# Latent projections of a diffusion trunk in another order, with norm work per kind

## The reference, cut to what matters

```python
def rmsnorm(x, g):
    y = xf * lax.rsqrt(jnp.mean(xf * xf, axis=-1, keepdims=True) + EPS)
    return (y * g.astype(jnp.float32)).astype(x.dtype)

def mla_queries(p_q, q_norm_g, w_uq):
    q = (rmsnorm(p_q, q_norm_g) @ w_uq).reshape(B, L, MLA_HEADS, QK_NOPE + QK_ROPE)

def mla_keys_values(p_kv, kv_norm_g, w_ukv):
    c_kv, k_rope = p_kv[..., :KV_LORA], p_kv[..., KV_LORA:]
    kv = (rmsnorm(c_kv, kv_norm_g) @ w_ukv).reshape(B, L, MLA_HEADS, QK_NOPE + V_DIM)
```

## Time and profile before

| What | Value |
|---|---|
| Median of 3 runs | 3062.06 us (3060.01 to 3062.21) |
| The profiled execution's own time | 3062.36 us |
| Its span in the profile | 3060.6 us |
| Mean granted TensorE clock | 0.928 of full |
| TensorE busy (matrix instructions) | 2575.2 us, 84% of the span |
| VectorE, ScalarE, GpSimd busy | 847.7, 610.4, 538.4 us |
| Latent projections, layer 0 | 528.0 to 613.0 us of the span |
| Latent projections, layer 1 | 1984.8 to 2056.7 us of the span |

### The profile page before, as it was taken

One profiled execution on the slowest core, in us unless ns is written; L12 is line 12 of the kernel. 1 busy time (PEld: TensorE's weight loads), 2 busy tenths in 40 slices (PEclk: granted clock), 3 DMA queues, 4 the chain that ended last, 5 costly groups with the idle time before them and its releaser, 6 DMA issues. The chain is left out here.

```text
span 3060.6 us, 33600 instructions
## 1 busy us (share of the span) xinstructions
PE 2575.2 (84%) x12474; PEld 1499.8 (49%) x12474; DVE 847.7 (28%) x1633; ACT 610.4 (20%) x1186; POOL 538.4 (18%) x500
## 2 busy tenths in 40 slices
PE   6987977899999995988888569789999869889881
PEld 2434655545565544555554244555544445555551
DVE  3553257134100135211111142614300341111113
ACT  3332210134100011211111131004300112111111
POOL 0000011046200001222221120106500012222222
PEclk8999998999999997999989789889999979999996
DMA  9663112001013325999999422102033469999992
GB/s 332 244 251 126 69 62 65 2 12 48 21 41 104 129 89 218 388 400 396 396 385 376 176 104 75 70 10 52 7 82 96 177 268 390 395 397 400 399 359 107
DMA packets 206731, 590.78 MB, mean 193 GB/s; under 512 B 47328, under 2 KB 104715, under 8 KB 156332
## 3 DMA queue, kind: packets, MB, share of 16 engines
q1 hardware_dynamic: 183029, 557.75, 48.9%
q0 software_dynamic: 22944, 31.52, 3.2%
q10 hardware_dynamic: 663, 0.27, 0.0%
HBM read 584.07 MB, written 51.51 MB: 208 GB/s over the span
## 5 line engine op out<-in xcount | busy, mean ns | idle before, releaser
L1907 PE MATMUL ps<-wgu,moe_xt 128*64 128x256 f32 x4096 | 512.8, 407 | 122.9 <-DMA wd<-in_w_down_e 120.5
L1907 PEld LDWEIGHTS ps<-wgu,moe_xt 128*64 128x64 f32 x4096 | 336.0, 146 | 256.0 <-issue 143.6
L1486 PE MATMUL ps<-u,w_merge 128*128 128x512 f32 (+1 forms) x768 | 281.8, 525 | 4.0 <-DVEq L1503 4.0
L2000 POOL DMA_INDIRECT rows_out<-moe_rows_out,table x128 | 118.6, 927 | 788.2 <-DVE moe_rows_out L2059 768.4
L1915 PE MATMUL ps<-wd,moe_ht 128*64 128x512 f32 x1024 | 247.8, 605 | 1.5 <-DVE moe_ht L2101 1.5
L2095 DVE TENSOR_TENSOR moe_gated<-ps,moe_gated 64x256 f32<-64x256 f32 x128 | 54.5, 426 | 594.9 <-ACT moe_gated L2078 581.6
L796 PE MATMUL ps<-u,w_hy 128*128 128x512 f32 (+1 forms) x576 | 209.4, 521 | 5.6 <-PEq L127 5.6
L1486 PEld LDWEIGHTS ps<-u,w_merge 128*128 128x128 f32 x768 | 146.8, 191 | 135.1 <-issue 123.6
L1243 POOL TENSOR_SCALAR attn_p<-attn_p,attn_rs 128x768 f32<-128x768 f32 (+1 forms) x80 | 155.3, 1949 | 81.3 <-DVE attn_rs L1412 80.9
L2078 ACT ACTIVATE moe_gated<-ps 64x256 f32<-64x256 f32 x128 | 48.2, 376 | 602.5 <-PE ps L1907 578.5
L2059 DVE COPY moe_rows_out<-ps 64x512 f32<-64x512 f32 x128 | 88.7, 693 | 267.1 <-PE ps L1915 267.1
(11 more groups left out here) (313 smaller groups left out, 3028.1 us busy)
## 6 DMA issues: line engine op xcount, KB each, us to landing
wgu<-in_w_gate_e SPq DMA_DIRECT2D x128, 1024.0 KB
wgu<-in_w_up_e SPq DMA_DIRECT2D x128, 1024.0 KB
wd<-in_w_down_e SPq DMA_DIRECT2D x128, 1024.0 KB
prep_w<-in_w_ada SPq DMA_DIRECT2D x24, 2048.0 KB
w_merge<-in_w_in SPq DMA_DIRECT2D x32, 512.0 KB, 5.2
w_hy<-in_w_in SPq DMA_DIRECT2D x6, 2048.0 KB
transfer<-prep_out POOLq DMA_DIRECT2D x10, 1024.0 KB, 9.4
h<-transfer SPq DMA_DIRECT2D x4, 2048.0 KB, 11.4
```

The source lines that it names most:

```text
L1486: last = nc.tensor.matmul(m.ps[:, bank, 0:n], w[:, b, w_at + c], z[:, c, at:at + n], start=c == 0, stop=c == kn - 1)
L1907: last = nc.tensor.matmul(ps[k * SLOTS:(k + 1) * SLOTS, 0:DE], xt[:, c], wgu[:, k, c], start=c == 0, stop=c == KC - 1)
L2000: nc.gpsimd.indirect_dma_start(out=dram["y"], out_offset=bass.IndirectOffsetOnAxis(ap=m.table[0:SLOTS, j:j + 1], axis=0), in_=y[:, j % 2], ...
```

## The change

The units come in the order key-values, queries, rotary key (`order`), and banks go by the place in that order. The key-values' sums stand after the first query unit, their rows after the last query unit. The rotary key's latent half comes next, then the queries' sums, then its context half, then the queries' rows. ScalarE takes one root per kind: that of the key-values between the second and the third query unit, that of the queries last. VectorE does mean, reciprocal root and diagonals of the key-values, then their normalised product, then the rotary key's latent part, then mean, reciprocal root and diagonals of the queries, the rotary key's context copies, and the queries' normalised product. The loads on SyncE's queue and the copies on GpSimd are as before.

```diff
--- before.py
+++ after.py
@@ -1027,6 +1027,7 @@
     NU = QC + KVC + 1
     tiles_of = [sum(n for _, _, n in streams_q) // P, TT]
     turns = [(k, j) for k in (1, 0) for j in range(tiles_of[k])]
+    order = (*range(QC, QC + KVC), *range(QC))
     src = w_in[l].rearrange("(c p) n -> p c n", p=P)
     w, w_loaded = early
     wv, wv_in = values
@@ -1035,6 +1036,8 @@
                [("wkr", [P, KC, P]), ("raw", [P, QC + KVC, TOK]),
                 ("sq", [P, QC + KVC, TOK]), ("r", [P, sum(tiles_of)]), ("var", [P, sum(tiles_of)]), ("tmp", [P, sum(tiles_of)]),
                 ("diag", [P, sum(tiles_of), P]), ("t", [P, 2, SEQ]), ("g", [P, QC])]) as (block, s):
+        NQ = tiles_of[0]
+
         def streams(i):
             return streams_q if i < QC else both
 
@@ -1067,7 +1070,7 @@
             def sums(k):
 
                 first, past = ((0, QC), (QC, QC + KVC))[k]
-                pe.wait_ge(s["sq_done"], past)
+                pe.wait_ge(s["sq_done"], (QC + KVC, KVC)[k])
                 for j in range(tiles_of[k]):
                     for c in range(first, past):
                         last = nc.tensor.matmul(m.ps[:, 4 + k, j:j + 1], s["sq"][:, c, j * P:(j + 1) * P], m.ones[:, 0:1],
@@ -1084,66 +1087,87 @@
                 last.then_inc(s["rows_done"], 1)
 
             pe.wait_ge(w_loaded, 16)
-            for i in range(NU):
-                if i >= 2:
-                    pe.wait_ge(s["sq_done"], i - 1)
-                    pe.wait_ge(s["raw_done"], i - 1)
-                if i == NU - 1:
-                    pe.wait_ge(s["swapped"], 4)
-                for t, at, n in streams(i):
+            for n, i in enumerate(order):
+                if n >= 2:
+                    pe.wait_ge(s["sq_done"], n - 1)
+                    pe.wait_ge(s["raw_done"], n - 1)
+                for t, at, size in streams(i):
                     for c in range(KC):
-                        lhs = w[:, c, i * P:(i + 1) * P] if i < NU - 1 else s["wkr"][:, c]
-                        last = nc.tensor.matmul(m.ps[:, 2 * (i % 2) + t, 0:n], lhs, m.u[:, c, at:at + n],
+                        last = nc.tensor.matmul(m.ps[:, 2 * (n % 2) + t, 0:size], w[:, c, i * P:(i + 1) * P], m.u[:, c, at:at + size],
                                                 start=c == 0, stop=c == KC - 1)
                 last.then_inc(s["mm_done"], 1)
-                if i in (QC, QC + KVC):
-                    sums(0 if i == QC else 1)
-            for k in (1, 0):
-                rows(k)
+                if n == KVC:
+                    sums(1)
+            rows(1)
+
+            pe.wait_ge(s["swapped"], 4)
+            pe.wait_ge(s["sq_done"], NU - 2)
+            pe.wait_ge(s["raw_done"], NU - 2)
+            for t, at, size in both:
+                for c in range(KC):
+                    last = nc.tensor.matmul(m.ps[:, 2 * ((NU - 1) % 2) + t, 0:size], s["wkr"][:, c], m.u[:, c, at:at + size],
+                                            start=c == 0, stop=c == KC - 1)
+                last.then_inc(s["mm_done"], 1)
+                if t == 0:
+                    sums(0)
+            rows(0)
 
         @block.scalar
         def _(act):
             nc.scalar.mul(s["g"][:], m.cols[:, l, R_QG:R_QG + QC], SCALE)
-            for i in range(NU - 1):
-                act.wait_ge(s["mm_done"], i + 1)
-                for t, at, n in streams(i):
-                    last = nc.scalar.activation(s["raw"][:, i, at:at + n], m.ps[:, 2 * (i % 2) + t, 0:n], ACT.Copy)
+            def root(turn, k):
+                act.wait_ge(s["dve"], 6 * turn + 1)
+                part = slice(k * NQ, k * NQ + tiles_of[k])
+                nc.scalar.activation(s["r"][:, part], s["var"][:, part], ACT.Sqrt).then_inc(s["root_done"], 1)
+
+            for n, i in enumerate(order):
+                act.wait_ge(s["mm_done"], n + 1)
+                for t, at, size in streams(i):
+                    last = nc.scalar.activation(s["raw"][:, i, at:at + size], m.ps[:, 2 * (n % 2) + t, 0:size], ACT.Copy)
                 last.then_inc(s["raw_done"], 1)
-                for t, at, n in streams(i):
-                    last = nc.scalar.activation(s["sq"][:, i, at:at + n], m.ps[:, 2 * (i % 2) + t, 0:n], ACT.Square)
+                for t, at, size in streams(i):
+                    last = nc.scalar.activation(s["sq"][:, i, at:at + size], m.ps[:, 2 * (n % 2) + t, 0:size], ACT.Square)
                 last.then_inc(s["sq_done"], 1)
-            act.wait_ge(s["dve"], 1)
-            nc.scalar.activation(s["r"][:], s["var"][:], ACT.Sqrt).then_inc(s["root_done"], 1)
+                if n == KVC + 1:
+                    root(0, 1)
+            root(1, 0)
 
         @block.vector
         def _(dve):
             link = Chain(dve, s["dve"])
-            NQ = tiles_of[0]
-            dve.wait_ge(s["sum_done"], 2)
-            for k, width in ((0, QL), (1, KVL)):
-                last = nc.vector.tensor_scalar(s["var"][:, k * NQ:k * NQ + tiles_of[k]], m.ps[:, 4 + k, 0:tiles_of[k]], 1.0 / width, EPS,
-                                               ALU.mult, ALU.add)
-            link(last)
-            dve.wait_ge(s["root_done"], 1)
-            refined_rsqrt(nc, link, s["r"][:], s["var"][:], s["tmp"][:])
-            for n, (k, j) in enumerate(turns):
-                nc.vector.tensor_scalar_mul(s["diag"][:, n], m.ident[:], s["r"][:, k * NQ + j:k * NQ + j + 1]).then_inc(s["diag_done"], 1)
-            for i in (*range(QC, QC + KVC), *range(QC)):
-                n = sum(n for _, _, n in streams(i))
-                k, out, g = (0, m.qn[:, i, 0:n], s["g"][:, i:i + 1]) if i < QC else \
-                    (1, m.kvn[:, i - QC, 0:n], m.cols[:, l, R_KVG + i - QC:R_KVG + i - QC + 1])
-                dve.wait_ge(s["rows_done"], 2 - k)
-                row = m.ps[:, (4, 6)[k]:(4, 6)[k] + 2].rearrange("p b n -> p (b n)")[:, 0:n]
-                nc.vector.scalar_tensor_tensor(out, row, g, s["raw"][:, i, 0:n], ALU.mult, ALU.mult).then_inc(s["norm_done"], 1)
+
+            def diagonals(turn, k):
+                part = slice(k * NQ, k * NQ + tiles_of[k])
+                dve.wait_ge(s["sum_done"], turn + 1)
+                link(nc.vector.tensor_scalar(s["var"][:, part], m.ps[:, 4 + k, 0:tiles_of[k]], 1.0 / (QL, KVL)[k], EPS, ALU.mult, ALU.add))
+                dve.wait_ge(s["root_done"], turn + 1)
+                refined_rsqrt(nc, link, s["r"][:, part], s["var"][:, part], s["tmp"][:, part])
+                for n, (kind, j) in enumerate(turns):
+                    if kind == k:
+                        nc.vector.tensor_scalar_mul(s["diag"][:, n], m.ident[:], s["r"][:, k * NQ + j:k * NQ + j + 1]).then_inc(s["diag_done"], 1)
+
+            def normalised(turn, k):
+                dve.wait_ge(s["rows_done"], turn + 1)
+                for i in (range(QC), range(QC, QC + KVC))[k]:
+                    n = sum(n for _, _, n in streams(i))
+                    out, g = (m.kvn[:, i - QC, 0:n], m.cols[:, l, R_KVG + i - QC:R_KVG + i - QC + 1]) if k else (m.qn[:, i, 0:n], s["g"][:, i:i + 1])
+                    row = m.ps[:, (4, 6)[k]:(4, 6)[k] + 2].rearrange("p b n -> p (b n)")[:, 0:n]
+                    nc.vector.scalar_tensor_tensor(out, row, g, s["raw"][:, i, 0:n], ALU.mult, ALU.mult).then_inc(s["norm_done"], 1)
 
             b = 2 * ((NU - 1) % 2)
+            diagonals(0, 1)
+            normalised(0, 1)
             dve.wait_ge(s["mm_done"], NU)
             dve.wait_ge(s["rope_in"], 16)
             nc.vector.tensor_tensor(s["t"][NOPE:QK, 0], m.ps[NOPE:QK, b], m.rope[NOPE:QK], ALU.mult)
             link(nc.vector.tensor_tensor(s["t"][NOPE:QK, 1], m.ps[QK:P, b], m.rope[QK:P], ALU.mult))
             for h in range(2):
                 nc.vector.tensor_tensor(m.key[QK:P, h, 0:SEQ], s["t"][NOPE:QK, 0], s["t"][NOPE:QK, 1], ALU.add)
+            diagonals(1, 0)
+            dve.wait_ge(s["mm_done"], NU + 1)
+            for h in range(2):
                 nc.vector.tensor_copy(m.key[NOPE:QK, h, SEQ:TOK], m.ps[NOPE:QK, b + 1, 0:CTX])
+            normalised(1, 0)
 
 
 def attention_loads(eng, l, i, a, early):
```

## The result

The changed kernel takes 3040.74 us, median of 4 runs (3038.7 to 3045.79), against 3062.14 us for the one before in the same comparison. The ratio is 0.9932 with a 95% interval of 0.9919 to 0.9944, so 17 to 25 us faster. Two later comparisons with five runs each gave 3043.45 us (ratio 0.9946, 0.9932 to 0.9959) and 3044.82 us (0.9938, 0.9924 to 0.9951), a gain of 17.8 us both times. The forecast was 3049.5 us with a range from 3044 to 3056: the direction was right, the size was not. The first two medians lie under the range, the third just inside it.

What follows compares the result with a forecast made beforehand. The projection stages were taken as bound by TensorE, then by VectorE's chain behind the last sums, not by loads. Gains of 5.2 (layer 0), 5.7 (layer 1) and 1.8 us (attention's starts), 12.7 together, gave 3049.5 us, range 3044 to 3056.

Steps and rivals of the forecast that it cites:

- the signs named: Layer 0: VectorE starting some 34 us after the first product, both rows without wait, about 3.8 us TensorE idle before attention.
- the reading by which a Square needs another table set than the root: ScalarE: each turn between Square and root would cost a table load; the prediction rejected it, costing the root 0.2 us hidden.
- second query unit 10.34 + 1.78: Layer 0, unit behind the key-values' sums: 10.34 us plain plus 1.78 us lost to the low clock.
- I take 2.1 here: Attention's start: assumed restart loss of 2.1 us instead of about 3.0, a gain of 0.9 us in each layer.
- The restarts after 3.74 and 4.88 us: Convolution blocks after these idle times lost 1.8 and 2.1 us; taken as the nearest rows for attention's start.
- the queries' rows at the middle of two prices: Rows behind the rotary context half: 2.0 us in layer 0 (ends 1.5, 2.5), 1.3 in layer 1 (ends 1.0, 1.7).
- the clock gives nothing away: Rival: sums between dense units leave the clock up, so 6.6 us go back; 3043 us, chance 0.15.
- its four losses: Clock losses behind both sets of sums: 1.78 us twice in layer 0, 1.50 us twice in layer 1.
- The clock falls more often: Rival: rows behind the third query unit pull the clock down again, 6.0 us together; 3055.5 us, chance 0.13.
- the clock stays down: Rival: low clock from first sums to last rows, 27.4 us in layer 0, about 21 in layer 1; 3098 us, chance 0.04.
- Hidden anyway: Rival: the stage shortens but a later stage waiting on loads gives it back; 3060 us, chance 0.06.
- its own better case: The rival in which the clock stays up behind the sums, giving back 6.6 us; 3043 us, chance 0.15.

Runs made afterwards that it cites:

- the moved sums: Changed kernel plus two unread 512-column products, some 1.7 us, ahead of the key-values' sums in both layers; 3044.13 us in one run.
- the kernel with the rotary key in one piece: Changed kernel with the rotary key's halves together again and the queries' sums behind both; 3050.01 us, ratio 0.9957, leaving out one run of 7190.65 us.
- layer 1's old stage: Layer 1's stage as before the change, seen in the kernel before (3061.21 us) and in the kernel with the new stage only in layer 0 (3052.74 us).
- the one-layer kernels: Kernel before with the new stage in one layer only: layer 0 3052.74 us (ratio 0.9972), layer 1 3052.53 us (ratio 0.9972).
- the filled one: Changed kernel plus four (layer 0) or three (layer 1) unread 512-column products behind the queries' rows, before attention; 3043.47 us.
- layer 0 alone: New stage in layer 0, the stage of the kernel before in layer 1; 3052.74 us against 3061.21, ratio 0.9972.
- the dealt-out kernel: Changed kernel with most sums placed singly between query units' dense products, only the queries' last third between the rotary halves; 3041.20 us, later 3043.62 us.

## Why the prediction missed

The mechanism was right. VectorE's chain stood behind the last sums and now lies beside TensorE's products; each of the signs named came true: VectorE's first instruction 33.8 us after the first product, rows behind the third query unit and behind the context half without a wait, 3.71 us of idle before attention, no wait on a diagonal. No table load stands in either stage, and the output stage keeps its two loads to ten roots, as in the earlier trace rows, so ScalarE's extra root brought no load and TensorE never waited for it. The same groups after the change:

```profile
L1621 ACT ACT_TABLE_LOAD x2 | 2.6, 1283 | 0.0
...
L1621 ACT ACTIVATE out_r<-out_var 128x1 f32<-128x1 f32 x10 | 2.0, 203 | 1.8 <-DVE out_var L1643 1.8
```

With two roots per stage among copies and squares, the reading by which a Square needs another table set than the root is out.

What was off is the size of the clock's terms in the sum:

| Term (us) | Layer 0: forecast, measured | Layer 1: forecast, measured |
|---|---|---|
| First three units | 31.02, 31.03 | 27.57, 27.58 |
| Key-values' sums | 2.86, 2.60 | 2.86, 2.84 |
| Two query units behind them | 22.46, 20.72 | 15.28, 15.26 |
| Key-values' rows | 1.5, 1.34 | 1.5, 1.34 |
| Rotary latent half | 6.89, 6.87 | 6.89, 6.87 |
| Queries' sums | 3.94, 3.94 | 2.86, 2.59 |
| Rotary context half | 5.21, 5.22 | 4.93, 5.23 |
| Queries' rows, multiplies, barrier | 5.83, 5.21 | 4.32, 3.97 |
| Stage | 79.7, 76.93 | 66.2, 65.68 |
| Gain at attention's start | 0.9, 1.09 | 0.9, 2.85 |

The step that failed is the clock's price, at two places above all. Three terms carry 4.7 of the 5.5 us between the forecast's 12.7 and the 18.2 that stages and starts show in the traces. First, "second query unit 10.34 + 1.78" in layer 0: nothing was lost, 1.7 us too much. It was taken from the only two rows at hand, both of which had the loss, and carried over as if it belonged to a set of sums; the moved sums show that it belongs to their place. Second, attention's start in layer 1: "I take 2.1 here", a loss, where the measured loss is nearly nothing (3.51 us for 3.4), 2.0 us too much. The restarts after 3.74 and 4.88 us stood for an idle time that the prediction itself put at 3.0 us, and it took the dearer of them. A price by length of idle time was the wrong kind of price as well: 2.92 us cost 0.1 us in the changed kernel and 2.1 in the kernel with the rotary key in one piece, and layer 1's old stage paid 1.6 after 6.83 us and 2.9 after 7.25. Third, the queries' rows at the middle of two prices, where the clock was back up and both layers paid the lower, 0.6 and 0.4 us. A slip without weight: by the rows used, the unit behind the sums lost 1.76 and 1.48 us, not 1.78 and 1.50.

The rival "the clock gives nothing away" named the right side but the wrong picture: of its four losses one vanished, and the others stayed at 1.5 to 1.8 us. "The clock falls more often" and "the clock stays down" found no row. "Hidden anyway" is refuted: the rest of the kernel lies between 2886.6 and 2893.0 us in the traces of the changed kernel, of the one-layer kernels and of the filled one, with 2891.1 before, and the two layers' gains add up. The range failed because it stopped at 3044 although its own better case was at 3043, and because it let only one of the clock's two places, the sums or the start, come out well.

The first comparison's 21.4 us remain above the 18.2 of the traces and the later 17.8. By 18.2 the time would be 3044.2 us, at the edge of the range, and 3 us of the first median have no cause here. Its interval holds both values, and the rest of the kernel lay between 4.5 us under and 1.9 us over that of before in these traces, so no cause is claimed for the difference.

## What to carry to other kernels

When two engines take turns behind a last product, give each kind of work its own short chain and put dense products between them; here that was worth 18 us of the 170 that the two stages and attention's starts took, and the rotary key's context half in the right gap was worth 5 to 7 of them. Price a light stretch of this kind on TensorE as nothing or 1.7 us, and a start after some us of idle time as anything from nothing to 2.9, each with a chance, and not at what the one row at hand shows; and let the range hold all of them coming out well. Products of the next stage can be put into the idle time before it. That gained nothing in one kernel here and 4.8 us by the medians in another, so measure whether what follows keeps the time.

## What was not expected of the hardware

The granted clock behind a stretch of 24 sums repeats from trace to trace and yet depends on its place. Four traces of the new stage in layer 0 (the changed kernel three times, and layer 0 alone) took 76.93, 76.94, 76.94 and 76.94 us, with starts that lay up to 2.9 us apart in the span. Moving the sums by 1.7 us within the stage did change it. So what counts is not the place in the span but the place behind something ahead in the kernel, and what that is no run here shows. The Trainium skill ("TensorE: Matmul & The Clock Gate", What's actually happening) says that the activity monitor runs by its own time and doesn't start with the kernel, so that the point of a clock change varies from run to run. In layer 0 these four traces show no such variation. In layer 1 there is a little: the sums, in which the clock begins to fall, took 2.84, 2.86 and 2.89 us in the three traces of the changed kernel and 2.60 in the filled one, but sums and query units together took 18.1 us every time, so the cost did not change.

A sum with one moving column costs 0.11 us at the full clock (2.60 us for 24) and 0.21 us at the low one (48 in 10 us). Between dense products it costs no more. The stretch of the dealt-out kernel that holds layer 0's two query units and their 48 sums:

```profile
557.50:583.50 26.00, 26.00 (x115) 17.50 (x113) 2.12 (x11) 3.37 (x9) 0.00 (x0) 1.00 0.00 1
```

Two plain units are 20.7 us, so 48 sums took some 5.2 us, 0.11 each, and the clock never fell.
